# Staggering the first two column tiles of an output projection on one Trainium2 core

## The chip, the cores and the metric

The kernel runs on one core of a Trainium2 chip. The metric is the time of one execution on the device in microseconds (us); a kernel's time is the median of its runs. A core has TensorE (PE, matmuls), VectorE (DVE), ScalarE (ACT), GpSimd (POOL) and SyncE (SP), which here only issues DMAs. The engines run side by side and wait for one another through semaphores. TensorE's clock has two levels here, 1.2 and 2.4 GHz; the profile shows the granted one as a share of the full one.

## What is computed

One layer of a decoder, for a prompt of 512 tokens and 8 sampled tokens, 520 columns in all, of width 2048. Attention and retention branches read the same normalised input; their outputs are projected, gated and merged, and the change is in what follows:

```python
merged = (jax.nn.sigmoid(ga) * jnp.einsum('bse,ed->bsd', ya, w_a_out)
          + jax.nn.sigmoid(gb) * jnp.einsum('bse,ed->bsd', yr, w_r_out))
y = jnp.einsum('bsd,de->bse', merged, w_o)
h = h + rms_norm(y, g_post)
h = h + jax.nn.sigmoid(jnp.einsum('bsd,de->bse', h, w_ple_gate)) * jnp.einsum('bsp,pd->bsd', p, w_ple_proj)
```

The change concerns the first two of the 16 column tiles of `y`.

## The kernel before

All large matrix products have one form. The result is made in column tiles of 128; such a tile is a **unit** (`unit`, L462 to L477). It runs over 16 k steps of 128 rows. Each operand is held as a high and a low part, so a k step is three passes (high by high, high by low, low by high) over two halves of 260 columns: 6 matmuls, 96 a unit. The stationary side is `W` ("weights" in the trace), the moving side `U` ("moving"), the sums go to `acc`. `W`, the raw weights `raw` and `acc` have two buffers each, and unit after unit takes them in turn, 0 and 1.

The units' weights come this way. SP loads `raw` for the unit after next as soon as the low split has read the buffer (L407). ACT makes the high part (`hi`, L798), DVE the low part (`lo`, L1095) and adds to `s_wready`, for which TensorE waits at a unit's start (L465). `hi` for the next use of a buffer comes on ACT after it has waited for the end of the unit that read the buffer (`s_unit`) and has taken that unit's sums out of `acc`.

The moving side of the output projection is the merged tensor `M`, 16 tiles (k steps) of 128x520. When the last unit of the projection before is done, DVE finishes `M` (L1528, L1532), ACT makes the high parts of the 16 tiles one by one (L1039), DVE the low parts (L1542), and each adds to `s_mov`. The split of the second unit's weights stands in the middle of these tiles, on ACT and DVE after tile 6 (L1040, L1543). The order on each engine is the order in which the code is written.

TensorE's first unit waits for each tile (`tiles_due`, L471), the second needs none of these waits; then a loop runs the other 14:

```python
unit(0, tiles_due={k: 1 for k in range(KD)})
unit(1)
with count.loop(KD // 2 - 1, rates, first=1) as i:
    for j in range(2):
        unit(j)
```

For each unit of this projection ACT reads the sums twice, as a copy (L1046) and as squares (L1048), then splits the next weights (`hi`, L798). DVE adds the squares to a running sum (L1553), then makes the low part (L1095).

The gate projection behind it starts with `pair` (L479 to L492): two units side by side, k step for k step, on tiles made on DVE's L1572. The second unit ends one step after the first. SP also issues copies of the caches (`keep_rows`, L373).

Of the kernel before, what the change touches and what calls it, by code (L numbers as in the profile page):

```python
# [28 lines left out]
KD = D // P  # L29
# [4 lines left out]
HC = TC // 2  # L34
# [55 lines left out]
def build(nc, x_prompt, x_sample, cache0, cache1, cache2, state, p_prompt, p_sample, g_pre, w_in, g_ret,  # L90
# [16 lines left out]
    def sem(name):  # L107
        return stack.enter_context(nc.semaphore(name))


    U = stack.enter_context(nc.sbuf_tensor("moving", [P, 2, KD, TC], F32R))
    W = stack.enter_context(nc.sbuf_tensor("weights", [P, 2, 2, KD, P], F32R))
# [10 lines left out]
    acc = stack.enter_context(nc.psum_tensor("acc", [P, 2, 2, 512], F32))  # L123
# [76 lines left out]
    def sems(name, n):  # L200
        return [sem(f"{name}{i}") for i in range(n)]
# [7 lines left out]
    s_wready = sem("weights_ready")  # L209
    s_unit = sem("unit_done")  # L210
    s_accfree = sems("acc_free", 2)
# [9 lines left out]
    s_mov = sem("moving_ready")  # L221
# [235 lines left out]
    def _(pe):  # L457
        count = Waits(pe)
        count.starts[id(s_wready)] = 2
        halfcols = [(0, HC), (HC, TC)]  # L460

        def unit(par, ks=tuple(range(KD)), hooks=None, tiles_due=None):  # L462


            pe.wait_ge(s_wready, count.due(s_wready))  # L465
            pe.wait_ge(s_accfree[par], count.due(s_accfree[par]))
            passes = [(0, 0), (0, 1), (1, 0)]
            for k in ks:
                for f in (hooks or {}).get(k, ()):
                    f()  # L470
                if tiles_due and k in tiles_due:  # L471
                    pe.wait_ge(s_mov, count.due(s_mov, skip=tiles_due[k] - 1))
                for n, (wp, up) in enumerate(passes):
                    for half, (a, b) in enumerate(halfcols):
                        mm = pe.matmul(acc[:, par, half, 0:HC], W[:, par, wp, k, :], U[:, up, k, a:b],  # L475
                                       start=(k == ks[0] and n == 0), stop=(k == ks[-1] and n == 2))
            mm.then_inc(s_unit, 1)  # L477
# [14 lines left out]
                        mm.then_inc(s_unit, 1)  # L492


        pe.wait_ge(s_ident, 16)
        fill = 0
        for tb in range(TB):
            pe.wait_ge(s_xload[tb], count.due(s_xload[tb]))
            for n0 in range(0, KD, 4):
                pe.wait_ge(s_free[fill % 4], count.due(s_free[fill % 4]))  # L500
                for n in range(4):
                    mm = pe.transpose(aux[:, fill % 4, n * P:(n + 1) * P],
                                      x_nat[:, tb, (n0 + n) * P:(n0 + n + 1) * P], ident[:])
# [4 lines left out]
        for n in range(KD):  # L508
            mm = pe.transpose(aux[:, 0, n * NS:(n + 1) * NS], xs_nat[0:NS, n * P:(n + 1) * P], ident[0:NS, 0:NS])
        mm.then_inc(s_full[0], 1)  # L510
        pe.wait_ge(s_xload[5], count.due(s_xload[5], skip=1))
        for j in range(2):
            pe.wait_ge(s_free[1 + j], count.due(s_free[1 + j]))
            for tb in range(TB):
                mm = pe.transpose(aux[:, 1 + j, tb * P:(tb + 1) * P], p_nat[:, tb, j * P:(j + 1) * P], ident[:])
            mm.then_inc(s_full[1 + j], 1)
        pe.wait_ge(s_free[3], count.due(s_free[3]))
        for j in range(2):
            mm = pe.transpose(aux[:, 3, j * NS:(j + 1) * NS], ps_nat[0:NS, j * P:(j + 1) * P], ident[0:NS, 0:NS])
# [11 lines left out]
        for n in range(KD):  # L531
# [3 lines left out]
            for k in range(2):  # L535
                for m, (wp, up) in enumerate([(0, 0), (0, 1), (1, 0)]):
                    for half, (a, b) in enumerate(halfcols):
                        mm = pe.matmul(acc[:, n % 2, half, 0:HC], W[:, n // 8, wp, 2 * (n % 8) + k, :],  # L538
                                       U[:, up, k, a:b], start=(k == 0 and m == 0), stop=(k == 1 and m == 2))
# [211 lines left out]
        with count.loop(KD // 2 - 1, rates, first=1) as i:  # L751
            for j in range(2):
                unit(j, ret_ks)
        unit(0, tiles_due={k: 1 for k in range(KD)})
        unit(1)
        with count.loop(KD // 2 - 1, rates, first=1) as i:
            for j in range(2):
                unit(j)
# [24 lines left out]
        for n in range(KD):  # L783
            if n % 4 == 0:
                pe.wait_ge(s_free[n // 4], count.due(s_free[n // 4]))
            mm = pe.transpose(aux[0:NS, n // 4, (n % 4) * P:(n % 4 + 1) * P], outS[:, n * NS:(n + 1) * NS], ident[:])
# [5 lines left out]
    def _(act):  # L792
        count = Waits(act)

        def hi(par, k=KD, loads=1):

            act.wait_ge(s_wload[par], count.due(s_wload[par], skip=loads - 1))
            act.activation(W[:, par, 0, 0:k], raw[:, par, 0:k], ACT.Copy).then_inc(s_whi, 1)  # L798
# [90 lines left out]
        with count.loop(H, [(s_unit, 10), (s_wload[0], 5), (s_wload[1], 5), (s_max, 4), (s_full[0], 7), (s_full[1], 7),  # L889
                        (s_full[2], 7), (s_full[3], 7)]) as h:  # L890
            for j in range(UNITS_ATT):
                par = j % 2
# [144 lines left out]
        for n in range(KD):  # L1037
            act.wait_ge(s_m, count.due(s_m))
            act.activation(U[:, 0, n, :], M[:, n, :], ACT.Copy).then_inc(s_uhi, 1)  # L1039
            if n == 6:  # L1040
                hi(1)
        mflat = M.rearrange("p n c -> p (n c)")
        with count.loop(KD // 2, [*proj_rates, (s_sqadd, 2)]) as i:
# [38 lines left out]
        for q in range(4):  # L1082
            act.wait_ge(s_full[q], count.due(s_full[q]))
            a = act.activation(osr[0:NS, q, 0:T], aux[0:NS, q, :], ACT.Copy)
# [4 lines left out]
    def _(dve):  # L1089
        count = Waits(dve)  # L1090

        def lo(par, k=KD):

            dve.wait_ge(s_whi, count.due(s_whi))
            dve.tensor_tensor(W[:, par, 1, 0:k], raw[:, par, 0:k], W[:, par, 0, 0:k].bitcast(F32),  # L1095
                              ALU.subtract).then_inc(s_wready, 1)
# [55 lines left out]
        for m in range(KD + 2):  # L1152
            if 4 <= m < KD:
                dve.wait_ge(s_mov, count.due(s_mov))
            if m < KD:
                k = U_KS[m]
                dve.scalar_tensor_tensor(out=utmp[:, m % 4, :], in0=xT[:, k, :], scalar=gpre[:, k:k + 1], in1=rstd,
                                         op0=ALU.mult, op1=ALU.mult).then_inc(s_u, 1)
            n = m - 2
            if n >= 0:  # L1160
                dve.wait_ge(s_uhi, count.due(s_uhi))
                dve.wait_ge(s_u, count.due(s_u))
                k = U_KS[n]
# [376 lines left out]
        for n in range(KD):  # L1540
            dve.wait_ge(s_uhi, count.due(s_uhi))
            dve.tensor_tensor(U[:, 1, n, :], M[:, n, :], U[:, 0, n, :].bitcast(F32), ALU.subtract).then_inc(s_mov, 1)  # L1542
            if n == 6:  # L1543
                lo(1)
        dve.memset(mean_d[:], 1.0 / D)
        dve.memset(sqsum, 0.0)
# [312 lines left out]
```

## Time and profile before

| | |
|---|---|
| time, median of 3 runs | 3151.82 us (3151.3 to 3155.41) |
| the profiled execution | 3152.52 us |
| its span, first to last instruction | 3151.0 us |
| TensorE busy | 3058.6 us, 97% of the span |
| DVE busy | 1158.1 us, 37% |
| ACT busy | 829.5 us, 26% |
| POOL busy | 371.0 us, 12% |
| mean granted clock of TensorE | 0.988 |

Times in the rows count from the start of the span. "PE L475" is a matmul written at line 475, "PEld" its weight load; a "q" behind an engine's name is its sequencer. The ends of matmuls are modelled, so that matmuls that follow closely overlap in the rows, and a group of them counts as busy from the first start to the last end. In a row of the timeline the bracket tells how long the engine was idle before it, and who ended that.

### The profile page before, as it was taken

How to read it: one execution, taken by the hardware profiler on the slowest of the kernel's cores; microseconds unless marked ns; L12 is line 12 of the kernel's file. 1: busy time of each engine (PE TensorE's matmuls, PEld its weight loads, DVE VectorE, ACT ScalarE, POOL GpSimd, SP SyncE). 2: the span in 40 equal slices, each digit the busy share in tenths (PEclk: the TensorE clock that was granted, in tenths of full speed). 3: DMA queues.
4: the chain of work that ended last, by engine and by line, in shares of the span. 5: the costliest groups of instructions: out<-in, count | busy, mean ns of one | idle time of the engine just before them, and what ended most of it. 6: DMA issues, size and time to landing. Idle time of an engine off the chain costs nothing.

```text
span 3151.0 us, 58535 instructions
## 1 busy us (share of the span) xinstructions
PE 3058.6 (97%) x24406; PEld 2982.6 (95%) x24406; DVE 1158.1 (37%) x1341; ACT 829.5 (26%) x985; POOL 371.0 (12%) x551
## 2 busy tenths in 40 slices
PE   7999999999999999999999999999999999999798
PEld 7999999999999999999999999999999999999798
DVE  4324233342423433443443453443211443422632
ACT  6222232222223222222222222222222221222322
POOL 2000000000000000220220220221000110100410
PEclk9999999999999999999999999999999999999899
DMA  9555656465564643654654654677665576655352
GB/s 312 192 181 189 201 173 214 160 203 191 189 208 150 208 149 121 182 161 134 194 155 125 197 154 127 192 231 249 208 210 173 164 246 207 227 183 173 107 172 83
DMA packets 534878, 574.84 MB, mean 182 GB/s; under 512 B 15512, under 2 KB 495576, under 8 KB 531480
## 3 DMA queue, kind: packets, MB, share of 16 engines
q1 hardware_dynamic: 490944, 428.31, 42.7%
q0 software_dynamic: 43744, 143.55, 14.2%
q8 instruction: 173, 2.83, 0.4%
q14 instruction: 17, 0.14, 0.0%
HBM read 515.54 MB, written 232.42 MB: 237 GB/s over the span
## 4 chain that ended last, share of the span: by engine, by line
PE 94%; DVE 2%; issue 1%; ACT 1%; DMA 1%; DVEq 0%; ACTq 0%; SPq 0%; POOL 0%; POOLq 0%
PE acc L475 84%; PE aux L556 1%; PE aux L578 1%; PE aux L625 1%; PE aux L635 1%; PE aux L644 1%; PE aux L694 1%; DVE stage_buffers L1568 1%; PE aux L567 1%; PE aux L547 1%; DMA stage_buffers<-in_x_prompt 0%; PE acc L538 0%; PE aux L618 0%; PE aux L652 0%; PE aux L685 0%
## 5 line engine op out<-in xcount | busy, mean ns | idle before, releaser
L475 PE MATMUL acc<-moving,weights 128*128 128x260 f32 x22080 | 2755.9, 285 | 36.7 <-issue 25.6
L475 PEld LDWEIGHTS acc<-moving,weights 128*128 128x128 f32 x22080 | 2687.5, 189 | 58.3 <-issue 45.9
L1095 DVE TENSOR_TENSOR weights<-raw_weights,weights 128x2048 fp32r<-128x2048 f32 (+1 forms) x242 | 538.8, 2226 | 1319.2 <-ACT weights L798 1305.2
L798 ACT ACTIVATE weights<-raw_weights 128x2048 fp32r<-128x2048 f32 (+1 forms) x242 | 450.9, 1863 | 214.2 <-PE acc L475 205.3
L873 ACT ACTIVATE stage_buffers<-acc 128x520 f32<-128x520 f32 x144 | 87.1, 605 | 1085.8 <-PE acc L475 1085.6
L1605 POOL DMA_DIRECT2D out<-stage_buffers x72 | 52.2, 725 | 672.1 <-DVEq L1178 499.8
L984 ACT ACTIVATE stage_buffers<-acc 128x520 f32<-128x520 f32 x32 | 19.4, 606 | 266.0 <-PE acc L475 257.2
L878 ACT ACTIVATE stage_buffers<-stage_buffers,small 128x384 f32<-128x384 f32 (+3 forms) x32 | 32.6, 1019 | 150.5 <-DVE small L1193 150.5
L885 ACT ACTIVATE stage_buffers<-aux 128x384 f32<-128x384 f32 (+2 forms) x72 | 35.4, 492 | 102.7 <-PE aux L567 102.7
L1683 POOL DMA_DIRECT2D out<-stage_buffers x64 | 45.5, 716 | 142.1 <-DVEq L1345 126.1
L1636 POOL DMA_DIRECT2D stage_buffers<-in_cache_win x24 | 21.7, 903 | 313.4 <-DVE sample_keep L1213 213.2
L1329 DVE SCALAR_TENSOR_TENSOR stage_buffers<-stage_buffers,sampled 128x256 f32<-128x256 f32 x128 | 52.1, 479 | 16.2 <-ACT stage_buffers L931 16.1
L1582 DVE TENSOR_TENSOR stage_buffers<-stage_buffers 128x520 f32<-128x520 f32 x16 | 11.2, 700 | 117.2 <-ACTq L1072 117.2
L1774 POOL TENSOR_TENSOR stage_buffers<-stage_buffers 128x520 f32<-128x520 f32 x16 | 27.0, 1697 | 218.9 <-DVE stage_buffers L1568 218.9
L1605 POOL DMA_DIRECT2D sg_scr<-stage_buffers x32 | 17.4, 543 | 300.6 <-ACTq L985 261.8
L1528 DVE TENSOR_TENSOR stage_buffers<-acc,stage_buffers 128x520 f32<-128x520 f32 x16 | 11.2, 700 | 112.1 <-PE acc L475 112.1
L1553 DVE TENSOR_TENSOR stage_buffers<-stage_buffers 128x520 f32<-128x520 f32 x16 | 11.2, 701 | 110.6 <-ACTq L1049 110.6
L556 PE MATMUL aux<-stage_buffers 128*128 128x128 f32 (+3 forms) x192 | 51.9, 406 | 0.0
L1187 DVE SCALAR_TENSOR_TENSOR stage_buffers<-stage_buffers,small,aux 128x128 f32<-128x128 f32 (+3 forms) x96 | 45.1, 510 | 11.0 <-PE aux L556 8.2
L1605 POOL DMA_DIRECT2D y_scr<-stage_buffers x24 | 13.1, 548 | 299.2 <-DVEq L1245 151.7
L578 PE MATMUL aux<-stage_buffers 128*128 128x256 f32 (+1 forms) x192 | 47.9, 406 | 0.0
L578 PEld LDWEIGHTS aux<-stage_buffers 128*128 128x128 f32 x192 | 33.4, 190 | 14.0 <-issue 7.7
(202 smaller groups left out, 1581.2 us busy)
## 6 DMA issues: line engine op xcount, KB each, us to landing
raw_weights<-in_w_in SPq DMA_DIRECT2D x176, 1024.0 KB, 6.1
out<-in_cache_win SPq DMA_DIRECT2D x128, 1023.5 KB, 8.4
out<-in_cache_win SPq DMA_DIRECT2D x32, 1022.0 KB, 8.0
out<-stage_buffers POOLq DMA_DIRECT2D x120, 256.0 KB, 3.3
stage_buffers<-in_cache_win POOLq DMA_DIRECT2D x48, 512.0 KB, 7.4
stage_buffers<-in_state_ret POOLq DMA_DIRECT2D x64, 256.0 KB, 6.2
raw_weights<-in_w_r_out SPq DMA_DIRECT2D x16, 1024.0 KB, 6.0
raw_weights<-in_w_o SPq DMA_DIRECT2D x16, 1024.0 KB, 5.9
```

Source lines behind the costliest of these rows:

```text
L475: mm = pe.matmul(acc[:, par, half, 0:HC], W[:, par, wp, k, :], U[:, up, k, a:b], start=(k == ks[0] and n == 0), stop=(k == ks[-1] and n == 2))
L556: pe.matmul(aux[:, g, 0:n], qT[:, g, q], kT[:, g, a:a + n], start=True, stop=True).then_inc(s_full[g], 1)
L578: mm = pe.matmul(aux[:, 3, a:z], v_nat[:, g, kb, :], PT[:, g, kb, a:z], start=(n == 0), stop=(n == len(parts) - 1))
L798: act.activation(W[:, par, 0, 0:k], raw[:, par, 0:k], ACT.Copy).then_inc(s_whi, 1)
L873: act.activation(halves(dst), acc[:, par, :, 0:HC], func, scale=scale).then_inc(ready, 1)
L878: act.activation(sc[b], sc[b], ACT.Exp, bias=negmax[:, b:b + 1], accum_out=den[:, b:b + 1]).then_inc(s_exp, 1)
L885: act.activation(PT[:, g0:g1, k0:k1, b * P:(b + 1) * P], src, ACT.Copy).then_inc(s_free[m % 3], 1)
L1095: dve.tensor_tensor(W[:, par, 1, 0:k], raw[:, par, 0:k], W[:, par, 0, 0:k].bitcast(F32), ALU.subtract).then_inc(s_wready, 1)
L1187: dve.scalar_tensor_tensor(out=sc[b][:, at:at + n], in0=dist[:, tab:tab + n], scalar=nslope[:, bass.ds(h + g * H, 1)], in1=aux[:, g, 0:n], ...
L1329: dve.scalar_tensor_tensor(out=r_st[:, half, b, j, :], in0=r_v[:, half, b, :], scalar=zs[:, bass.ds(h * 2 * NS + at, 1)], in1=r_st[:, half ...
L1605: pool.dma_start(dst, src).then_inc(stored, 16)
L1683: pool.dma_start(ret_s[0, half * HB + b, bass.ds(h, 1)].rearrange("o (j p) e -> p (o j) e", p=P), r_st[:, half, b]).then_inc(s_rnewst[half ...
```

## The change

TensorE runs the first two units of the output projection interleaved, from a new function `staggered(3)`. The first unit takes step k as soon as its tile is there; the second takes step k - 3 right after it, from k = 3 on, and its last three steps stand alone at the end. TensorE asks for the second unit's weights and sum buffer after the first unit's step 3. ACT and DVE split the second unit's weights after tile 2 instead of tile 6. Nothing else differs.

```diff
+        def staggered(lag):
+
+            def step(par, k):
+                for n, (wp, up) in enumerate([(0, 0), (0, 1), (1, 0)]):
+                    for half, (a, b) in enumerate(halfcols):
+                        mm = pe.matmul(acc[:, par, half, 0:HC], W[:, par, wp, k, :], U[:, up, k, a:b],
+                                       start=(k == 0 and n == 0), stop=(k == KD - 1 and n == 2))
+                if k == KD - 1:
+                    mm.then_inc(s_unit, 1)
+
+            pe.wait_ge(s_wready, count.due(s_wready))
+            pe.wait_ge(s_accfree[0], count.due(s_accfree[0]))
+            for k in range(KD + lag):
+                if k < KD:
+                    pe.wait_ge(s_mov, count.due(s_mov))
+                    step(0, k)
+                if k == lag:
+                    pe.wait_ge(s_wready, count.due(s_wready))
+                    pe.wait_ge(s_accfree[1], count.due(s_accfree[1]))
+                if k >= lag:
+                    step(1, k - lag)
...
-        unit(0, tiles_due={k: 1 for k in range(KD)})
-        unit(1)
+        staggered(3)
         with count.loop(KD // 2 - 1, rates, first=1) as i:
...
             act.activation(U[:, 0, n, :], M[:, n, :], ACT.Copy).then_inc(s_uhi, 1)
-            if n == 6:
+            if n == 2:
                 hi(1)
...
             dve.tensor_tensor(U[:, 1, n, :], M[:, n, :], U[:, 0, n, :].bitcast(F32), ALU.subtract).then_inc(s_mov, 1)
-            if n == 6:
+            if n == 2:
                 lo(1)
```

How the instructions stand on TensorE at the end of the two units and the loop's entry, before ("moving_ready" is a tile, "weights_ready" a low split, L465 and L466 the waits of `unit`):

```order
L475 MATMUL acc<-moving,weights 128x260 [waits moving_ready]
L475 MATMUL acc<-moving,weights 128x260 x5
L475 MATMUL acc<-moving,weights 128x260 [waits acc_free1,weights_ready]
L475 MATMUL acc<-moving,weights 128x260 x95
L335 UNCONDITIONAL_BRANCH
L335 ISA
L466 REGISTER_ALU [waits weights_ready]
L475 MATMUL acc<-moving,weights 128x260 [waits acc_free0]
```

The same place after the change (L500 is the matmul of `staggered`):

```order
L500 MATMUL acc<-moving,weights 128x260 [waits moving_ready]
L500 MATMUL acc<-moving,weights 128x260 x11
L500 MATMUL acc<-moving,weights 128x260 [waits moving_ready]
L500 MATMUL acc<-moving,weights 128x260 x29
L335 UNCONDITIONAL_BRANCH
L335 ISA
L466 REGISTER_ALU [waits weights_ready]
L475 MATMUL acc<-moving,weights 128x260 [waits acc_free0]
```

Between the last wait for a tile and the loop there stood 6 + 96 matmuls, and now 30: the first unit's last 6, then 24 of the second.

On DVE, from the last tile of the projection before, the order was this (L1542 is a tile's low part, L1095 a low split of weights):

```order
L1528 TENSOR_TENSOR stage_buffers<-acc,stage_buffers 128x520 [waits gate_in_loaded1,unit_done]
L1532 TENSOR_TENSOR stage_buffers<-stage_buffers 128x520
L1542 TENSOR_TENSOR moving<-stage_buffers,moving 128x520 [waits moving_hi] x7
L1095 TENSOR_TENSOR weights<-raw_weights,weights 128x2048 [waits weights_hi]
L1542 TENSOR_TENSOR moving<-stage_buffers,moving 128x520 [waits moving_hi] x9
```

After the change, with the new line numbers (21 or 22 higher):

```order
L1549 TENSOR_TENSOR stage_buffers<-acc,stage_buffers 128x520 [waits gate_in_loaded1,unit_done]
L1553 TENSOR_TENSOR stage_buffers<-stage_buffers 128x520
L1563 TENSOR_TENSOR moving<-stage_buffers,moving 128x520 [waits moving_hi] x3
L1116 TENSOR_TENSOR weights<-raw_weights,weights 128x2048 [waits weights_hi]
L1563 TENSOR_TENSOR moving<-stage_buffers,moving 128x520 [waits moving_hi] x13
```

The low split now stands ahead of tile 3 instead of tile 7. ACT's order changes in the same way.

## Rows read from the trace of the kernel before

**Rows 1.** The page: busy time, the chain that ended last, the costliest group.

```profile
PE 3058.6 (97%) x24406; PEld 2982.6 (95%) x24406; DVE 1158.1 (37%) x1341; ACT 829.5 (26%) x985; POOL 371.0 (12%) x551
...
PE 94%; DVE 2%; issue 1%; ACT 1%; DMA 1%; DVEq 0%; ACTq 0%; SPq 0%; POOL 0%; POOLq 0%
PE acc L475 84%; PE aux L556 1%; PE aux L578 1%; PE aux L625 1%; PE aux L635 1%; PE aux L644 1%; PE aux L694 1%; DVE stage_buffers L1568 1%; PE aux L567 1%; PE aux L547 1%; DMA stage_buffers<-in_x_prompt 0%; PE acc L538 0%; PE aux L618 0%; PE aux L652 0%; PE aux L685 0%
...
L475 PE MATMUL acc<-moving,weights 128*128 128x260 f32 x22080 | 2755.9, 285 | 36.7 <-issue 25.6
```

**Rows 2.** Timeline, projection's start: start us, us, what, count [idle before].

```profile
2714.50 0.39 SPq L407 DMA_DIRECT2D raw_weights<-in_w_o  x1
...
2721.57 3.80 ACT L1039 ACTIVATE moving<-stage_buffers 128x520 fp32r<-128x520 f32 x7 [9.61 <-PE acc L475]
...
2723.15 4.36 DVE L1542 TENSOR_TENSOR moving<-stage_buffers,moving 128x520 fp32r<-128x520 f32 x7
...
2724.00 36.19 PE L475 MATMUL acc<-moving,weights 128*128 128x260 f32 x288 [2.47 <-DVE moving L1542]
2725.27 1.90 ACT L798 ACTIVATE weights<-raw_weights 128x2048 fp32r<-128x2048 f32 x1
...
2727.43 2.28 DVE L1095 TENSOR_TENSOR weights<-raw_weights,weights 128x2048 fp32r<-128x2048 f32 x1
2729.63 5.57 DVE L1542 TENSOR_TENSOR moving<-stage_buffers,moving 128x520 fp32r<-128x520 f32 x9
...
2737.26 0.61 ACT L1046 ACTIVATE stage_buffers<-acc 128x520 f32 x1 [5.35 <-PE acc L475]
...
2738.54 1.92 ACT L798 ACTIVATE weights<-raw_weights 128x2048 fp32r<-128x2048 f32 x1 [0.18 <-issue]
2740.49 2.29 DVE L1095 TENSOR_TENSOR weights<-raw_weights,weights 128x2048 fp32r<-128x2048 f32 x1 [1.36 <-ACT weights L798]
...
2748.80 0.60 ACT L1046 ACTIVATE stage_buffers<-acc 128x520 f32 x1 [8.34 <-PE acc L475]
```

**Rows 3.** Windows: stretch, its us, PE busy (count), granted clock, DMA share, GB/s.

```profile
2721.52:2723.44 1.92, 0.01 (x1) 1.00 1.95 603
2723.44:2724.00 0.56, 0.00 (x1) 0.50 1.17 432
2724.00:2726.86 2.86, 2.86 (x13) 0.50 0.21 81
2726.86:2730.30 3.44, 3.44 (x31) 1.00 0.00 0
```

**Rows 4.** DMA issues from 2702.9 on: count, KB, median us to landing.

```profile
raw_weights<-in_w_o SPq DMA_DIRECT2D x1, 1024.0 KB, 16.6
```

**Rows 5.** Timeline and windows behind the pair of the gate projection.

```profile
2953.83 6.32 PE L489 MATMUL acc<-moving,weights 128*128 128x260 f32 x48 [0.62 <-DVE moving L1572]
...
2959.47 0.60 ACT L1071 ACTIVATE stage_buffers<-acc 128x520 f32<-128x520 f32 x1 [2.55 <-PE acc L489]
...
2962.15 2.29 DVE L1095 TENSOR_TENSOR weights<-raw_weights,weights 128x2048 fp32r<-128x2048 f32 x1
...
2964.50 5.24 PE L475 MATMUL acc<-moving,weights 128*128 128x260 f32 x24 [4.35 <-DVE weights L1095]
...
2962.38:2964.50 2.12, 0.00 (x1) 0.50 0.44 126
2964.50:2969.20 4.70, 4.70 (x21) 0.50 0.67 191
2969.20:2972.00 2.80, 2.80 (x26) 1.00 1.13 431
```

**Rows 6.** Timeline and windows of TensorE around six other idle gaps.

```profile
15.00 1.97 PE L502 MATMUL aux<-ident,stage_buffers 128*128 128x128 f32 x16 [3.06 <-DMA stage_buffers<-in_x_prompt]
...
15.00:20.40 5.40, 3.93 (x32) 1.00 1.07 302
...
2442.99 7.27 PE L475 MATMUL acc<-moving,weights 128*128 128x260 f32 x46 [2.40 <-DVE moving L1484]
...
2443.55:2446.96 3.41, 3.41 (x18) 0.50 0.27 50
...
1262.80 0.42 PE L666 MATMUL aux<-ident,sample_keep 128*64 128x128 f32 x1 [2.68 <-DVEq L1364]
...
1262.80:1269.37 6.57, 6.57 (x30) 0.50 0.27 93
...
1715.62 6.58 PE L475 MATMUL acc<-moving,weights 128*128 128x260 f32 x40 [1.82 <-issue]
...
1716.51:1719.92 3.41, 3.41 (x18) 0.50 0.00 1
...
1485.86 6.34 PE L475 MATMUL acc<-moving,weights 128*128 128x260 f32 x51 [1.96 <-issue]
...
1485.86:1495.00 9.14, 9.14 (x76) 1.00 0.40 117
...
2086.67 5.55 PE L475 MATMUL acc<-moving,weights 128*128 128x260 f32 x44 [1.86 <-DVE weights L1095]
...
2086.67:2095.00 8.33, 8.33 (x69) 1.00 0.87 265
```

## The prediction, made before the changed kernel was run

> **What bounds the kernel now.** I read the page's busy shares and chain first: TensorE is busy 97% of the span, the chain of waits that ended last is 94% TensorE, and it lies on L475, the matmul of a unit, with 84% [rows 1]. So only what makes TensorE wait, or run at its lower clock, can move the end. ACT and DVE, which split weights and tiles into a high and a low part, have slack in the mean (26% and 37%). They matter only where one of their steps ends last.
>
> The change sits at the start of the output projection. The timeline of that place [rows 2] reads so. TensorE is idle for 2.47 us until DVE has tile 0, then works from 2724.00 on without any idle piece that the timeline shows. ACT takes the first unit's sums (L1046) at 2737.26 and the second's at 2748.80. The second unit thus takes 11.54 us: 96 matmuls of 0.120 us, and one k step of a unit (6 matmuls) is 0.72 us. ACT's read begins some 0.3 us after the unit's last matmul has taken its slot (a matmul is 285 ns long by the page [rows 1] but holds a slot of 120 ns, which leaves 0.16, and the signal takes the rest). So the first unit holds TensorE from 2724.00 to about 2736.96, that is 12.96 us, 1.42 us more than the second.
>
> Where does the 1.42 go? The windows [rows 3] show it: the granted clock is at its lower level, 1.2 of 2.4 GHz, from 2723.44 to 2726.86, and TensorE works for 2.86 us of it at half speed, a loss of 1.43 us. Nothing is left for waits on tiles. DVE makes a tile in 0.61 us (7 in 4.36, one being 0.69 long [rows 2]), faster than TensorE uses one. DVE's only hole is the low split of the second unit's weights, 2727.43 to 2729.71, after tile 6. Tile 7 is ready at 2729.63 + 0.69 = 2730.32. TensorE, with 12 matmuls done by 2726.86 and 30 more to go to tile 7, wants it at 2726.86 + 3.6 = 2730.46. The hole fits to within a tenth.
>
> **The change, part by part.**
>
> 1. *The first wait.* Tile 0 depends on ACT and DVE steps that stay as they are. The 2.47 us and the low clock behind it stay.
>
> 2. *The split moves up.* ACT's high split of the second unit's weights needs their load, issued at 2702.97 and landed 16.6 us later, at 2719.6 [rows 4]; no new wait on DMA. With tiles 0.53 us apart on ACT (7 in 3.80 [rows 2]) it begins at 2721.57 + 3 x 0.53 = 2723.16 and ends, 1.90 later, at 2725.06. DVE ends tile 2 at 2723.15 + 2 x 0.61 + 0.69 = 2725.06, so the low split starts at 2725.09 (0.03 after ACT, as at 2740.49 [rows 2]). Tile 3 starts 2.20 later (as 2727.43 to 2729.63), at 2727.29, and ends at 2727.98; TensorE starts 0.15 after a tile (2723.84 to 2724.00), so at 2728.13. TensorE wants tile 3 after 18 matmuls: 12 by 2726.86 and 6 x 0.12, at 2727.58. **New wait: 0.55 us.** The hole that was hidden before tile 7 is now in front of tile 3, with only three steps of work as cover. Had the clock been full, the cover would be shorter (TensorE at tile 3 at 2726.2), but tile 7 would then be late before too, and both ends are set by DVE; the difference stays about 0.55.
>
> 3. *The stagger.* The second unit needs its low split at 2728.13 + 0.72 = 2728.85; it is ready at 2727.38. After that TensorE uses a tile every 1.44 us and DVE makes one in 0.61: no wait. The instructions are the same 192 matmuls and the same waits, in another order, 29 steps of 0.721 from 2728.13: both units end at 2749.05 instead of 2748.50, the 0.55 of before. The stagger itself gives nothing back, because there was no wait on tiles to fill.
>
> 4. *The handover to the loop.* This is the dear part. The first unit's last step is now the 25th of those 29, so it ends at 2728.13 + 25 x 0.721 = 2746.16, only 4 steps (2.88 us) before the second. Before, a whole unit (11.54 us) lay between. The loop's first unit takes its weights from the buffer that the first unit has just read, and they can be split into it only after that read. That chain starts with the first unit's end: ACT reads the sums twice (copy and square), then splits high; DVE adds squares, then splits low. From the start of L1046 to the end of L1095 it is 2740.49 + 2.29 - 2737.26 = 5.52 us [rows 2]; add 0.3 in front and 0.06 behind. Before, this lay under the 11.54 us. Now: 2746.16 + 0.3 + 5.52 + 0.06 = 2752.04, while TensorE is free at 2749.05. **New wait: 2.99 us**, on L1095. Its load is not late (issued at 2714.50, long landed). Behind the waiting matmul stands the whole rest of the projection, and nothing fills the gap. The same shape is in this trace: the gate projection starts as an interleaved pair, and the unit behind it waits 4.35 us for L1095 [rows 5]. There the first unit ends one step ahead (0.72), and from ACT's read at 2959.47 to TensorE's start at 2964.50 are 5.03 us; the output projection's chain is 0.55 longer for the second read, and the stagger covers 2.16 more: 4.35 + 0.55 - 2.16 = 2.74 us of idle time, beside 2.99 - 0.16 = 2.83 from the sum. After the loop's first unit all is 11.54 us apart again, and nothing is given back.
>
> 5. *The clock.* After idle gaps of 2.40 (2440.59), 2.47 (2721.53), 2.68 (1260.12) and 4.35 us (2960.15) the granted clock fell to 1.2 GHz every time; after 1.82 (ending at 1715.62) it fell, after 1.96 and 1.86 it did not, nor at once after 3.06 at the kernel's start, ending at 15.00 [rows 3, 5, 6]. The new gap of 2.99 us less the 0.16 by which a matmul outlasts its slot, 2.8 us, is nearest to those where it fell. The price lies between 1.43 us (the low stretch of [rows 3], its start still idle) and 1.71 (half of the 3.41 us at 2443.55 with TensorE working all through [rows 6]); I take 1.5. The Trainium skill, "TensorE: Matmul & The Clock Gate", section "HAM oscillation — how this bites in real kernels", warns only of idle gaps of TensorE longer than this one; by it the clock would hold and the sum lose its 1.5. The trace disagrees: the clock fell after 2.40 us.
>
> **Sum.** 0.55 + 2.99 + 1.5 = 5.0 us slower. The profiled execution took 3152.52 us (span 3151.0), 0.7 above the median of 3151.82; the difference is added to the median: **3156.8 us**.
>
> **Rivals.**
>
> *The clock holds.* The gap falls so that the clock stays at 2.4 GHz, as it did after 1.96 and 3.06 us. For it: falls do not follow the length of the gap alone. Against: four of the five gaps from 2.40 to 4.35 us that step 5 lists. Only 0.55 + 2.99 = 3.5: 3155.3 us.
>
> *The clock falls for two stretches, and the kernel is measurably slower.* At the pair the clock was low for 6.83 us from 2962.38 to 2969.20 [rows 5], and 6.83 us from 1262.54 [rows 6], with 4.70 and 6.57 us of work in them. If the new gap does the same, with up to 1 us of the low stretch idle, 5.8 to 6.8 us of work run at half speed: 2.9 to 3.4 us. Sum 6.4 to 6.9: 3158.5 us. It decides as soon as a second low stretch follows. Against it: the pair's gap was longer, and the one at 1260 stood among small matmuls.
>
> *The handover is covered.* If ACT and DVE were done with the weights when TensorE comes, only the 0.55 would be left: 3152.4 us. That needs a chain of 2.9 us where the rows show 5.9.
>
> *A gain.* If timed executions lose more on tiles than this profile shows, the stagger could fill it. All that the first unit has to give is 1.42 us: 3150.4 us. Against: the clock explains all of it.
>
> **How the numbers follow.** Forecast 60%, clock holds 21%, two low stretches 12%, handover covered 5%, gain 2%. About 0.2% (6.3 us) is what a measurement of this kernel can tell from no change; the runs of before spread from 3151.3 to 3155.41. The forecast's 5.0 is below 6.3, but the spread carries about one in six of its cases over it; with the second rival that makes slower 0.22. A gain of 6.3 has no source: faster 0.02, same 0.76. The range leaves out the last two rivals (7%) and the high end of the second: 3153.8 to 3159.4.
>
> **What the changed profile would show.** TensorE waits 0.5 to 0.7 us for DVE's tile 3 some 4 us after tile 0. ACT reads the first unit's sums near 2746.5, the second's 3 us later. TensorE then waits about 3 us for L1095's successor at the loop's entry, and a stretch at 1.2 GHz follows. Wrong would be: no wait at the loop's entry (step 4), tiles reaching TensorE late in the first unit of before (step 3), or the clock at full level after the gap (step 5).

## The result, and the profile after

The changed kernel takes 3160.26 us (median of 20 runs, 3153.64 to 3165.36), the kernel before 3154.73 us (20 runs now, 3146.91 to 3161.10). The ratio is 1.0018 with a 95% interval of 1.0012 to 1.0024: 5.7 us slower by the ratio, between 3.8 and 7.6, and 5.5 between the two medians. So the change costs about what was forecast (5.0), but 3160.26 lies 0.86 us above the stated range. The three runs known before gave a median of 3151.82; twenty give 2.9 us more. One of the 11 runs of the changed kernel in the experiments (4211.48 us) and one of the 29 of the kernel before beside it (3774.23 us) were in a much slower state; the ratios leave them out.

The profiled execution took 3160.88 us, its span is 3159.3 (before: 3152.52 and 3151.0). The page's first part after the change, beside [rows 1]:

```profile
PE 3063.7 (97%) x24406; PEld 2986.2 (95%) x24406; DVE 1158.1 (37%) x1341; ACT 829.6 (26%) x985; POOL 371.1 (12%) x551
```

DVE, ACT and the number of matmuls have not moved; TensorE is busy 5.1 us longer and idle 3.2 us longer. The timeline of the output projection's start, the rows that answer to [rows 2] (`staggered` is L500, and the other lines have gone up: L1067 is ACT's read L1046, L1116 the low split L1095, L819 the high split L798, L1060 a tile's high part L1039, L1563 its low part L1542):

```profile
2723.91 1.69 ACT L1060 ACTIVATE moving<-stage_buffers 128x520 fp32r<-128x520 f32 x3 [9.62 <-PE acc L475]
...
2726.34 2.37 PE L500 MATMUL acc<-moving,weights 128*128 128x260 f32 x18 [2.47 <-DVE moving L1563]
...
2727.44 2.29 DVE L1116 TENSOR_TENSOR weights<-raw_weights,weights 128x2048 fp32r<-128x2048 f32 x1
2729.65 8.02 DVE L1563 TENSOR_TENSOR moving<-stage_buffers,moving 128x520 fp32r<-128x520 f32 x13
...
2730.40 21.11 PE L500 MATMUL acc<-moving,weights 128*128 128x260 f32 x174 [1.69 <-DVE moving L1563]
...
2748.78 0.61 ACT L1067 ACTIVATE stage_buffers<-acc 128x520 f32 x1 [14.51 <-PE acc L500]
...
2752.01 2.29 DVE L1116 TENSOR_TENSOR weights<-raw_weights,weights 128x2048 fp32r<-128x2048 f32 x1 [1.36 <-ACT weights L819]
...
2754.43 20.74 PE L475 MATMUL acc<-moving,weights 128*128 128x260 f32 x158 [2.92 <-DVE weights L1116]
...
2767.86 0.60 ACT L1067 ACTIVATE stage_buffers<-acc 128x520 f32 x1 [12.88 <-PE acc L475]
```

The windows at the new gap and behind it (stretch, its us, busy and count for PE, PEld, DVE, ACT, POOL, then granted clock, DMA share, GB/s):

```profile
2751.51:2754.43 2.92, 0.00 (x1) 0.00 (x1) 2.29 (x1) 2.81 (x4) 0.00 (x0) 1.00 0.00 0
...
2755.61:2759.02 3.41, 3.41 (x18) 3.41 (x17) 1.76 (x1) 0.00 (x0) 0.00 (x0) 0.50 0.91 252
```

Whole runs of this kernel differ by many microseconds, so I read a stretch **S** in every profile: from ACT's first high tile of the output projection to ACT's read of the third unit's sums. It holds all that the change touches and, behind it, one whole unit. Before, it ends at

```profile
2760.32 0.60 ACT L1046 ACTIVATE stage_buffers<-acc 128x520 f32 x1 [8.39 <-PE acc L475]
```

so S is 2760.32 - 2721.57 = 38.75 us. After, it is 2767.86 - 2723.91 = 43.95: 5.2 us more. Of them 3.6 are there when the loop's first unit starts (30.52 us after ACT's first high tile, against 26.93 before, worked out as 2748.80 less the 0.3 of the prediction), and 1.6 come with that unit, which runs partly at 1.2 GHz.

### The profile page after: what moved, and what is told of

The parts are those of the page before. It is cut to its first block, busy times and chain, and to the rows that moved or that the text cites. A ratio compares the mean times of both kernels' runs of the same rounds, so it can differ in the third digit from the quotient of the medians.

```text
span 3159.3 us, 58535 instructions
## 1 busy us (share of the span) xinstructions
PE 3063.7 (97%) x24406; PEld 2986.2 (95%) x24406; DVE 1158.1 (37%) x1341; ACT 829.6 (26%) x985; POOL 371.1 (12%) x551
## 3 DMA queue, kind: packets, MB, share of 16 engines
q8 instruction: 173, 2.83, 0.4%
## 4 chain that ended last, share of the span: by engine, by line
PE 94%; DVE 2%; issue 1%; ACT 1%; DMA 1%; DVEq 0%; ACTq 0%; SPq 0%; POOL 0%; POOLq 0%
PE acc L475 83%; PE aux L578 1%; PE aux L600 1%; PE aux L647 1%; PE aux L657 1%; PE aux L666 1%; PE aux L716 1%; DVE stage_buffers L1589 1%; PE aux L589 1%; PE aux L569 1%; PE acc L500 1%; PE aux L640 0%; PE aux L674 0%; PE acc L560 0%; PE aux L707 0%
## 5 line engine op out<-in xcount | busy, mean ns | idle before, releaser
L475 PE MATMUL acc<-moving,weights 128*128 128x260 f32 x21888 | 2736.1, 285 | 37.5 <-issue 25.7
L1116 DVE TENSOR_TENSOR weights<-raw_weights,weights 128x2048 fp32r<-128x2048 f32 (+1 forms) x242 | 538.8, 2226 | 1314.6 <-ACT weights L819 1299.5
L819 ACT ACTIVATE weights<-raw_weights 128x2048 fp32r<-128x2048 f32 (+1 forms) x242 | 450.9, 1863 | 213.4 <-PE acc L475 204.4
L1350 DVE SCALAR_TENSOR_TENSOR stage_buffers<-stage_buffers,sampled 128x256 f32<-128x256 f32 x128 | 52.1, 479 | 16.0 <-ACT stage_buffers L952 15.9
```

The costliest lines, as they stand in the source:

```text
L1350: dve.scalar_tensor_tensor(out=r_st[:, half, b, j, :], in0=r_v[:, half, b, :], scalar=zs[:, bass.ds(h * 2 * NS + at, 1)], in1=r_st[:, half ...
```

## The experiments

All ran beside the kernel before, on the same chip as the others of their group. Edits are against the changed kernel unless said otherwise.

| kernel | lag, split after tile | gap at the loop's entry, us | clock fell behind it | S, us | median, us (runs) |
|---|---|---|---|---|---|
| before | none, 6 | 0 | - | 38.75 | 3154.73 (20) |
| before, again | none, 6 | 0 | - | 38.72 | 3158.07 (1) |
| early split alone | none, 2 | 0 | - | 39.32 | 3155.61 (12) |
| lag 0 | 0, 2 | 5.07 | yes | 49.33 | 3168.78 (5) |
| changed kernel | 3, 2 | 2.92 | yes | 43.95 | 3160.26 (20) |
| changed kernel, again | 3, 2 | 2.92 | yes | 43.80 | 3162.88 (11) |
| lag 3, late split | 3, 6 | 2.92 | yes | 44.95 | 3161.22 (1) |
| lag 5 | 5, 2 | 1.51 | no | 40.95 | 3160.43 (1) |
| lag 8 | 8, 2 | 0 | - | 39.20 | 3155.53 (11) |
| lag 8, late split | 8, 6 | 0 | - | 38.81 | 3155.30 (11) |
| tiles 0 to 3 first | none, 6 | 0 | - | 39.46 | 3156.79 (1) |
| late merge | 8, 8 (ACT 7) | 0 | - | 38.06 | 3152.42 (12) |
| late merge, mended | 8, 8 | 0 | - | 37.44 | 3156.57 (12) |

The kernel before had a median of 3154.33 us beside the first group (changed kernel again, early split alone, lag 0, lag 8), 3154.33 beside the second (lag 3 and lag 8 with the late split, tiles 0 to 3 first, late merge) and 3156.12 beside the third (before again, lag 5, late merge mended). The two kernels with 20 runs ran beside each other. A median is compared with that of its group; one that rests on a single run says nothing, and there S alone counts.

### The changed kernel again

> The changed kernel itself, as the yardstick of this chip. The stretch S runs from ACT's first high tile to ACT's read of the third unit's sums: 38.75 us in the profile of before, 43.95 in that of after, of which 1.71 by the lower clock after the new idle gap. Theory (early split 0.55, handover 2.99, clock 0 or 1.4 to 1.7): S is 42.3 if the clock holds and 43.7 to 44.0 if it falls; the whole time is 3.5 to 7 us above before. Rival (the loss is a matter of where clock falls happen to lie, not of this place): S would come back near 38.8 in some execution.

S was 2771.92 - 2728.12 = 43.80 us, with a fall at the loop's entry. The ratio to the kernel before was 1.0016 (1.0007 to 1.0025). Here the clock had also fallen behind the first gap, so TensorE came to tile 3 slowly and waited only 0.17 us for it, against 1.69 in the profile above:

```profile
2730.55 3.88 PE L500 MATMUL acc<-moving,weights 128*128 128x260 f32 x18 [2.47 <-DVE moving L1563]
...
2734.61 21.12 PE L500 MATMUL acc<-moving,weights 128*128 128x260 f32 x174 [0.17 <-DVE moving L1563]
...
2758.65 16.64 PE L475 MATMUL acc<-moving,weights 128*128 128x260 f32 x125 [2.92 <-DVE weights L1116]
```

Both go on 6.5 us after ACT's first high tile (2734.61 - 2728.12 and 2730.40 - 2723.91). The size of a wait alone tells nothing here; its end does, and DVE sets it.

### Lag 8: the handover

```diff
-        staggered(3)
+        staggered(8)
```

> Only the stagger's lag is changed, from 3 to 8 k steps. Theory of the handover: the first unit now ends 9 steps (6.5 us) before the second, more than the 5.9 us from its end to its successor's weights, so the wait of 2.9 us on the low split at the loop's entry is gone and with it the clock fall behind it; the early split's cost stays: S = 38.75 + 0.55 = 39.3 us. Rival (two units interleaved run slower by themselves, through alternating weights and sums): S stays above 42.

S was 2762.95 - 2723.75 = 39.20 us, and the row at the loop's entry has no wait any more:

```profile
2744.98 0.61 ACT L1067 ACTIVATE stage_buffers<-acc 128x520 f32 x1 [10.89 <-PE acc L500]
2748.21 2.29 DVE L1116 TENSOR_TENSOR weights<-raw_weights,weights 128x2048 fp32r<-128x2048 f32 x1 [1.36 <-ACT weights L819]
...
2751.12 19.14 PE L475 MATMUL acc<-moving,weights 128*128 128x260 f32 x158
```

The low split ends at 2750.50, 0.62 us before TensorE comes (2751.12). The instructions are the same; only the lag differs, and 4.7 us of the 5.2 are gone. The rival that interleaving is slow by itself falls. The ratio to the kernel before was 1.0002 (0.9993 to 1.0011).

### Lag 0 and lag 5: the wait goes with the lag

```diff
-        staggered(3)
+        staggered(0)
```

> Lag 0: both units side by side. Theory of the handover: the first unit ends one step (0.72 us) ahead, so the wait at the loop's entry is 5.88 - 0.72 = 5.16 us, 5.0 as idle time; TensorE also waits for the second unit's low split right after step 0. Worked out from tile 0 as before: low split ready at 5.87 us after ACT's first high tile, 31 steps from there, the loop's first unit starts 33.4 us after it against 26.9 before: S = 45.2 with the full clock, 47 to 48.5 with one or two falls. Rival (the wait at the entry is a fixed cost of leaving such a block, not a matter of lag): the wait stays at 2.9 and S at 42 to 44.

```profile
2731.34 24.11 PE L500 MATMUL acc<-moving,weights 128*128 128x260 f32 x186 [2.11 <-DVE weights L1116]
...
2760.53 19.67 PE L475 MATMUL acc<-moving,weights 128*128 128x260 f32 x142 [5.07 <-DVE weights L1116]
...
2774.80 0.60 ACT L1067 ACTIVATE stage_buffers<-acc 128x520 f32 x1 [13.71 <-PE acc L475]
```

The gap is 5.07 us, where 5.0 were expected. S is 49.33, 0.8 above the end of what was expected. The clock was low twice for 6.8 us, the second time from 1.5 us before the gap's end on (busy counts are TensorE's):

```profile
2731.34:2735.09 3.75, 3.75 (x17) 0.50 0.56 151
...
2760.53:2765.81 5.28, 5.28 (x24) 0.50 1.14 370
```

Half of 3.75 and of 5.28 is 4.5 us, where 3.3 stood in the upper end of what was expected; without them S is 44.8, where 45.2 was expected. In the whole time lag 0 is slower than before by 0.37% (0.24 to 0.50), 11.7 us.

The same edit with 5:

> Lag 5. Theory of the handover: the wait on the low split at the loop's entry is 5.88 - 6 x 0.721 = 1.55 us, seen as 1.5 idle; S = 38.75 + 0.55 + 1.55 = 40.85, and 42.3 to 42.6 if the clock falls. Rival (the wait doesn't go with the lag): 2.9.

```profile
2732.93 21.05 PE L500 MATMUL acc<-moving,weights 128*128 128x260 f32 x174 [0.31 <-DVE moving L1563]
...
2755.49 14.79 PE L475 MATMUL acc<-moving,weights 128*128 128x260 f32 x121 [1.51 <-DVE weights L1116]
...
2767.40 0.60 ACT L1067 ACTIVATE stage_buffers<-acc 128x520 f32 x1 [10.15 <-PE acc L475]
```

Gap and S (40.95) are as expected, and the clock stayed at its upper level behind a gap of 1.51 us. With 5.07, 2.92, 1.51 and 0 us for lags of 0, 3, 5 and 8, the idle time is, to within 0.12 us, the chain of 5.88 us less 0.72 for each step by which the first unit ends ahead (lag + 1 of them) and less the 0.16 by which a matmul outlasts its slot.

### The early split, alone and left out

Against the kernel before, on ACT and DVE:

```diff
-            if n == 6:
+            if n == 2:
```

> The kernel before with the split of the second unit's weights after tile 2 instead of 6, and no stagger. Theory: TensorE waits 0.5 to 0.7 us for tile 3 where the clock is low behind tile 0, about 1.7 where it is full, and the two units end 0.55 us later in both cases; S = 39.3. Rival (tile 7's wait before cost nothing only by luck, and moving the hole is free): S = 38.75 or less. The whole time is within 0.1% of before for both; the stretch decides.

```profile
2728.81 36.45 PE L475 MATMUL acc<-moving,weights 128*128 128x260 f32 x301 [0.32 <-DVE moving L1542]
...
2761.65 0.60 ACT L1046 ACTIVATE stage_buffers<-acc 128x520 f32 x1 [8.40 <-PE acc L475]
```

S is 2761.65 - 2722.33 = 39.32 us, 0.57 above 38.75: the forecast's 0.55. The row shows 0.32 us idle; with the 0.16 by which a matmul outlasts its slot that is 0.48, just under the 0.5 to 0.7 expected. The whole time can't tell (1.0001, 0.9992 to 1.0010).

The other way round, the stagger of 3 with the split left after tile 6 (`n == 2` to `n == 6`):

> The changed kernel with the split left after tile 6. Theory: TensorE waits after step 3 for the second unit's low split, ready 8.14 us after ACT's first high tile, and goes on with 28 steps; the loop's first unit starts 8.20 + 24 x 0.721 + 5.88 = 31.4 us after it (26.9 before, 30.5 with the early split): S = 43.2 with the full clock, 44.6 to 44.9 with a fall. So with lag 3 the early split is right, by 0.9 us. The wait at the loop's entry stays 2.9. Rival (the early split is what costs): S below 42.2.

```profile
2731.51 20.39 PE L500 MATMUL acc<-moving,weights 128*128 128x260 f32 x168 [1.37 <-DVE weights L1116]
...
2754.82 15.46 PE L475 MATMUL acc<-moving,weights 128*128 128x260 f32 x114 [2.92 <-DVE weights L1116]
```

S is 44.95 in the one profile, 1.0 to 1.2 more than with the early split, where 0.9 was worked out. So with a lag of 3 the early split is the better place for it; the stagger is what costs.

### Lag 8 without the early split: what the stagger gives

> Lag 8 and the split after tile 6 as before the change: the stagger without either of the two new waits. Theory: nothing is gained, since the stagger has no wait on tiles to fill, and nothing is lost: S = 38.75 us plus or minus 0.1, whole time as before. Rival (staggering does give something back once its waits are gone): S 38.3 or less.

S is 2765.69 - 2726.88 = 38.81 us, that of the kernel before within 0.1. Freed of both costs, this stagger gives nothing back. It does not show that no stagger could: at lag 8 the second unit's first step comes after tile 8, so it can't stand where TensorE may have to wait, for tile 7; and at lag 3 the second unit's weights are themselves what DVE is making in that hole. The ratio was 0.9994 (0.9985 to 1.0003).

### Before, again: is a wait on tiles hidden by the clock?

> The kernel before once more, for a second profile. Theory for the spread of whole runs: it is made of stretches at 1.2 GHz whose number varies (11 to 15 before the place of the change in ten profiles), so ACT's first high tile of the output projection starts at 2654.5 (plus or minus 1) + TensorE's idle time up to there (49 to 52 us) + half of TensorE's busy time at 1.2 GHz; S is 38.75 again whether or not the clock falls behind the first gap. Rival: the start of the projection moves by several us with the same number of low stretches.

```profile
2730.18 5.30 PE L475 MATMUL acc<-moving,weights 128*128 128x260 f32 x42 [2.47 <-DVE moving L1542]
...
2736.57 33.63 PE L475 MATMUL acc<-moving,weights 128*128 128x260 f32 x278 [1.08 <-DVE moving L1542]
...
2766.47 0.60 ACT L1046 ACTIVATE stage_buffers<-acc 128x520 f32 x1 [8.40 <-PE acc L475]
```

This time the clock stayed up behind tile 0, and TensorE did wait 1.08 us, for tile 7. S is 38.72, the same. With the split after tile 6 the low clock behind the first gap is free: it eats what would be a wait for tile 7. The first unit can't end sooner than DVE's queue up to tile 7 allows. That queue holds the split. Without a stagger the second unit needs it only a whole unit later, so a split after tile 15 might save up to 1.4 us with the full clock. That is an estimate which no run here tests: 2.43 to TensorE's start, 3 x 11.54 and 0.3 are 37.35, and DVE would be done with the split 13.7 us after ACT's first high tile (1.58 + 15 x 0.61 + 0.69 + 2.29), where the second unit wants it at 13.97.

The start of the projection, 2727.75, was worked out less well; that is taken up below.

### Tiles first

Against the kernel before: DVE makes the low parts of tiles 0 to 3 ahead of its last merge.

```diff
+                if last and j == 1:
+                    for n in range(4):
+                        low_tile(n)
...
+        for n in range(4, KD):
+            low_tile(n)
```

> The kernel before with one change: DVE makes the low parts of tiles 0 to 3 ahead of its two steps for the last merged tile. TensorE can start 0.9 us earlier, 1.5 us after ACT's first high tile instead of 2.43. Theory (where the clock doesn't decide, DVE's queue up to tile 7 sets the end of the first unit, not tile 0): DVE idles 0.6 us for ACT at the start, tile 7 comes 0.6 to 0.7 us later, and S = 39.4 although TensorE starts earlier. Rival (the first idle gap sets the end): S = 37.9, the 0.9 us gained.

```profile
2725.20 3.80 ACT L1039 ACTIVATE moving<-stage_buffers 128x520 fp32r<-128x520 f32 x7 [9.61 <-PE acc L475]
2725.94 2.53 DVE L1526 TENSOR_TENSOR moving<-stage_buffers,moving 128x520 fp32r<-128x520 f32 x4 [8.03 <-ACT moving L1039]
2726.79 3.09 PE L475 MATMUL acc<-moving,weights 128*128 128x260 f32 x24 [1.62 <-DVE moving L1526]
...
2730.72 2.44 PE L475 MATMUL acc<-moving,weights 128*128 128x260 f32 x18 [0.84 <-DVE moving L1526]
...
2734.76 35.42 PE L475 MATMUL acc<-moving,weights 128*128 128x260 f32 x293 [1.60 <-DVE moving L1526]
```

(L1526 is a tile's low part in this kernel.) TensorE starts 1.59 us after ACT's first high tile instead of 2.43, and still S is 39.46, 0.7 longer. The idle time has only been cut in three, 4.06 us in all, against 2.47 + 1.08 in the second profile of before. DVE stood idle for ACT's first tile (it starts at 2725.94, not at 2725.20), and tile 7 comes that much later.

### A faster version

Lag 8; DVE takes the last sums out of `acc`, makes tiles 0 to 8, splits, and adds the last merged tile after tile 11; ACT splits high after tile 7. The diff shows DVE's lines; `staggered(8)` and ACT's `n == 7` stand beside them:

```diff
+                if last and j == 1:
+                    return
                 dve.drain()
                 mt = mflat[:, bass.ds((2 * i + j) * TC, TC)]
...
-            if n == 2:
+            if n == 8:
                 lo(1)
+            if n == 11:
+                dve.drain()
+                dve.tensor_tensor(M[:, KD - 1, :], M[:, KD - 1, :], tmp, ALU.add).then_inc(s_m, 1)
```

> A version meant to be faster than both: lag 8; DVE takes the last sums out of acc, then makes tiles 0 to 8, then the low split, and adds the last merged tile only after tile 11 (ACT splits high after tile 7). Theory: tile 0 is there 0.8 us earlier (TensorE starts 1.6 us after ACT's first high tile), the hole of the low split lies where TensorE has the second unit's steps, and only the wait for the low split itself after step 8 is left, about 0.5 us: the low split is ready 8.5 us after ACT's first high tile, 23 steps follow: S = 8.6 + 23 x 0.721 + 11.54 + 0.3 = 37.0 with the full clock, 37.9 if it falls behind the first idle gap. Gain 0.8 to 1.7 us, which only the stretch can show. Rival (the start is bound by DVE in any order): S = 38.75.

S was 38.06, 0.7 shorter than before but above the 37.0 to 37.9 expected, and this with the full clock, where 37.0 was: I had put ACT's high split ahead of its tile 8 and not counted that DVE then waits for that tile. The rows show it (L1564 is a tile's low part in this kernel):

```profile
2726.19 0.70 DVE L1564 TENSOR_TENSOR moving<-stage_buffers,moving 128x520 fp32r<-128x520 f32 x1 [1.06 <-ACT moving L1060]
...
2729.14 16.74 PE L500 MATMUL acc<-moving,weights 128*128 128x260 f32 x138 [1.22 <-DVE weights L1116]
```

With ACT's split after tile 8 too:

> The faster version, mended: in the last one ACT made the high split ahead of tile 8, so DVE stood idle for 1.06 us for that tile and the low split came at 9.6 us instead of 8.5. Here ACT splits after tile 8 too: low split from 6.73 to 9.02 us after ACT's first high tile, S = 9.1 + 23 x 0.721 + 11.54 + 0.3 = 37.5 us with the full clock, 37.9 if the clock falls behind the first idle gap. Rival (DVE's total work binds, in any order of ACT's steps): S stays at 38.06. The whole time is 1 us below before, which 5 rounds can't tell from nothing.

```profile
2732.90 6.72 PE L500 MATMUL acc<-moving,weights 128*128 128x260 f32 x54 [1.55 <-DVE moving L1564]
...
2740.43 16.72 PE L500 MATMUL acc<-moving,weights 128*128 128x260 f32 x138 [0.80 <-DVE weights L1116]
...
2768.82 0.60 ACT L1067 ACTIVATE stage_buffers<-acc 128x520 f32 x1 [8.40 <-PE acc L475]
```

S is 2768.82 - 2731.38 = 37.44 us, at the full clock, where 37.5 was worked out: 1.3 less than before, 6.5 less than the changed kernel. How much of it is the stagger's is not shown, since the late merge was not run without it. An estimate from the rows: DVE makes tile 9 from 2740.29 to 2740.98, so that without the second unit's steps TensorE would go on some 0.6 us later than it did (2740.43). By that a little over half of the 1.3 us belongs to the late merge. In the whole time it is no more than the measurement: 0.9999 (0.9990 to 1.0007), and 0.9998 (0.9989 to 1.0007) for the version before it. It is faster by its stretch, not shown faster as a whole.

## Why the prediction was right in its steps and wrong in its time

**Steps 1 and 2** held. The first gap is again 2.47 us. TensorE goes on with tile 3 at 6.49 us after ACT's first high tile; 2728.13 - 2721.57 = 6.56 was worked out (it took 0.15 from a tile to TensorE's start, the row has 0.06). The early split alone costs 0.57 against 0.55. The wait seen in the changed profile (1.69) is larger than the forecast 0.55 because the clock had not fallen behind tile 0; the text had said that the difference stays, and the second profile of before, with its 1.08 us for tile 7, shows why.

**Step 3** held as far as it was tested: lag 8 with the split left in place is 38.81 against 38.75. Its reason, that there was no wait on tiles to fill, holds only where the clock is low behind tile 0; in the second profile of before there was one, of 1.08 us.

**Step 4** held: ACT's read of the first unit at 24.87 us (24.89 worked out), the loop's first unit at 30.52 (30.47), a gap of 2.92 (2.83). Lags of 0, 5 and 8 move it as the sum says.

**Step 5** held in kind and nearly in size. The clock fell in or behind the 2.92 us gap in all three profiles that have it (the changed kernel twice, and lag 3 with the late split). The price was 1.6 us in the first, where 1.5 was taken. Lag 5 gives a closer yardstick, a unit that starts after a wait and keeps the full clock: 11.91 us from its start to ACT's read (2755.49 to 2767.40). With a fall it took 13.43, 13.27 and 13.44, so a fall costs 1.4 to 1.5 us. By the Trainium skill, "TensorE: Matmul & The Clock Gate", section "HAM oscillation — how this bites in real kernels", it would have held, since the gap is shorter than those the section warns of; the three profiles here show otherwise. Of the rivals, the second (two low stretches) was seen with lag 0 alone, with its gap of 5.07 us.

**The step that failed** is the last one, "the difference is added to the median". The sum was right within what was measured: 5.0 us forecast, 5.5 between the medians (3.8 to 7.6), 5.2 and 5.05 in S. But it was added to 3151.82, the median of three runs, as if that were known to a few tenths. The text named the spread of those runs, 3151.3 to 3155.41, and used it for the chances but not for the base. Twenty runs put the base at 3154.73, with 3159.7 as the time forecast, and the range would have been 3156.7 to 3162.3. The medians beside the experiments (3154.33, 3156.12) agree with the later base. Of all choices of three out of the twenty runs, one in five has a median below 3152.68, low enough for 3160.26 to fall outside a range laid around it in the same way; the miss is partly the luck of that draw.

Two smaller points. The text says that the range leaves out the high end of the second rival; that end is 3151.82 + 6.9 = 3158.7, inside 3159.4. And it takes 6.3 us as what can be told from no change; twenty runs of each kernel gave 1.9 us on either side, and told the 5.7 from no change.

**Why the base spreads** can be read from the profiles. The output projection starts at another time in each, long before anything that the change touches. I added up TensorE's busy time in stretches at 1.2 GHz up to that start, from the granted clock and the matmuls of the trace, and took half of it as lost:

| profile | start of the projection, us | half of the busy time at 1.2 GHz | idle | the rest |
|---|---|---|---|---|
| late merge | 2719.49 | 13.8 | 50.4 | 2655.4 |
| before | 2721.57 | 15.5 | 51.4 | 2654.7 |
| changed kernel | 2723.91 | 18.6 | 50.4 | 2654.9 |
| changed, again | 2728.12 | 22.2 | 52.1 | 2653.9 |
| late merge, mended | 2731.38 | 25.4 | 52.4 | 2653.6 |
| before, again | 2727.75 | 22.5 | 48.0 | 2657.3 |

Five of the six agree within 1.8 us in the rest, while the starts lie 12 us apart: the spread is mostly time at 1.2 GHz, which the same gaps bring in one execution and not in another. The profile of before had the least of it but one in thirteen (late merge had less, late merge mended the most). The expectation for the sixth (2654.5 plus or minus 1) missed by 2.8 us. That is made in the first 30 us, where TensorE is busy longer in it and idle less: first the kernel before, then the same kernel again.

```profile
0.00:30.00 30.00, 13.41 (x97) 0.89 0.88 234
```

```profile
0.00:30.00 30.00, 16.50 (x96) 0.93 0.88 234
```

The mean clock of these windows misleads: the profile's record of it begins at 9.8 us in the first and at 18.8 us in the second, and the time ahead of that counts as full. How long the same 16 matmuls take shows the rate, at first in the kernel before, then in the same kernel again:

```profile
18.43 1.97 PE L502 MATMUL aux<-ident,stage_buffers 128*128 128x128 f32 x16 [1.47 <-DMA stage_buffers<-in_x_prompt]
```

```profile
10.68 3.68 PE L502 MATMUL aux<-ident,stage_buffers 128*128 128x128 f32 x16 [0.65 <-DMA stage_buffers<-in_x_prompt]
```

So the sixth ran its first matmuls at half rate for 9 us longer. With half of TensorE's busy time ahead of the record taken off too (1.8 us in before, 5.5 in the sixth), the rest is 2652.9 and 2651.7, and in all thirteen profiles it lies between 2651.7 and 2653.1.

## What to carry to other kernels

Two units in turn on two buffers hide the refill of one buffer under the whole of the other unit. Whoever interleaves them moves their ends together, and has then to ask what refills the first buffer and how long that takes: the first unit ends lag + 1 steps ahead, and these must be at least that chain (5.9 us here, 8.2 steps, so a lag of 8), or the interleaving costs the difference, and at lags of 3 and 0 here a clock fall as well. A step that hides behind tile 7 can be late before tile 3; and before a wait on tiles is worked on, look whether it is a wait at all, or the lower clock. Where three runs spread by as much as the effect, the base belongs in the range with its own width.

## What the runs showed of the hardware that was not expected

The same gap, at the same place and of the same length (2.46 or 2.47 us, ahead of tile 0), had a fall of TensorE's clock to 1.2 GHz in it or close behind it in seven of the ten profiles that have it, and none in three. In the three profiles in which it was cut to 1.55 or 1.62 us no fall followed. Such falls cost nothing where DVE was late anyway (38.75 and 38.72 us for S with and without), and 1.4 to 1.6 us where TensorE was the only one late.

Over the thirteen profiles a longer gap has a fall more often. Of the gaps from 40 us on that began at the full clock, with no other idle piece of over 0.5 us in the 7 us before them, a fall came, in the gap or behind it and ahead of the next such piece, in none of 53 gaps of 1.3 to 1.7 us, 16 of 55 of 1.7 to 2.2, 19 of 23 of 2.3 to 2.5 and all 16 of 2.6 to 3.0.
